# A bidirectional trunk layer on one Trainium2 core: expert weights in 4 MB transfers with eleven chunks fetched ahead, the next gather inside the last down projection, split memory products, narrower clock products

## The reference, cut to what matters

```python
x = LN1(alpha*x + hybrid_mixer(x, w_in, rpb, conv_w, w_out))   # windowed attention + short convolution
x = LN2(alpha*x + memory_cross_attention(x, mem, wq, wk, wv, wo))
x = LN3(alpha*x + expert_choice_moe(x, w_router, w_gate, w_up, w_down))

def memory_cross_attention(x, mem, wq, wk, wv, wo):
    k, v = mem @ wk, mem @ wv                  # (256 x 1024) @ (1024 x 512), twice
...
def expert_choice_moe(x, w_router, w_gate, w_up, w_down):
    affinity = softmax(x @ w_router)           # 512 x 16
    gates, idx = top_k(affinity.T, 64)         # every expert takes its 64 best tokens
    xe = x[idx]                                # 16 x 64 x 1024
    hid = silu(xe @ w_gate) * (xe @ w_up)      # per expert 1024 x 2048, twice
    ye = (hid @ w_down) * gates                # per expert 2048 x 1024
    return scatter_add(idx, ye)
```

## Time and profile before

| | us |
|---|---|
| median of 3 runs | 1283.73 (1283.42 to 1283.82) |
| the profiled execution | 1284.64 |
| its span, first to last instruction | 1282.8 |
| TensorE busy | 1173.8 (92%) |
| VectorE, ScalarE, GpSimd busy | 266.6, 183.3, 117.9 |
| SP's DMA queue, share of 16 engines | 82.0%, 440.84 MB |

### The profile page before, as it was taken

The page is one execution under the profiler, slowest core; times in us unless marked ns, Lnnn a source line. Parts: engine busy times, 40 slices in busy tenths (PEclk is TensorE's granted clock), DMA queues, the critical chain, the costliest instruction groups (busy, mean ns, idle before and its releaser), DMA issues.

```text
span 1282.8 us, 13692 instructions
## 1 busy us (share of the span) xinstructions
PE 1173.8 (92%) x5738; PEld 584.2 (46%) x5738; DVE 266.6 (21%) x488; ACT 183.3 (14%) x338; POOL 117.9 (9%) x59
## 2 busy tenths in 40 slices
PE   8999998999999999999889978997998899789995
PEld 6886776888743343333224322432432243224321
DVE  2012376726710020020002002000200020021114
ACT  4223344133000000000000001000000000000002
POOL 3412324430003000000000000000000000000002
PEclk8999999999999999999999999999999999999998
DMA  9422213048679999999999999999999999999994
GB/s 369 168 87 111 75 69 153 16 199 343 274 287 427 425 428 427 427 430 427 428 429 427 430 428 426 430 428 430 428 427 430 427 427 431 426 429 426 428 426 164
DMA packets 37858, 444.63 MB, mean 347 GB/s; under 512 B 5568, under 2 KB 5952, under 8 KB 10560
## 3 DMA queue, kind: packets, MB, share of 16 engines
q1 hardware_dynamic: 35232, 440.84, 82.0%
q10 hardware_dynamic: 2592, 3.29, 0.8%
HBM read 442.02 MB, written 2.10 MB: 346 GB/s over the span
## 4 chain that ended last, share of the span: by engine, by line
PE 74%; DMA 17%; DVE 5%; ACT 2%; issue 1%; POOL 0%; SPq 0%; DVEq 0%; ACTq 0%
PE bank L1169 25%; DMA ring<-in_w_exp 16%; PE bank L1208 15%; PE bank L1066 5%; PE bank L1218 4%; PE bank L749 2%; PE bank L751 2%; PE bank L754 2%; PE bank L738 2%; ACT yt L694 1%; PE bank L1195 1%; PE bank L1117 1%; PE bank L891 1%; PE bank L893 1%; PE bank L760 1%
## 5 line engine op out<-in xcount | busy, mean ns | idle before, releaser
L1169 PE MATMUL bank<-ring,yt 128*64 128x512 f32 x2048 | 453.1, 595 | 38.0 <-DMA ring<-in_w_exp 38.0
L1169 PEld LDWEIGHTS bank<-ring,yt 128*64 128x64 f32 x2048 | 142.8, 137 | 329.4 <-issue 255.9
L1208 PE MATMUL bank<-ring,yt 128*64 128x512 f32 x928 | 206.6, 596 | 26.7 <-ACT yt L694 20.9
L1208 PEld LDWEIGHTS bank<-ring,yt 128*64 128x64 f32 x928 | 67.0, 137 | 147.6 <-issue 113.9
L1554 DVE TENSOR_TENSOR work<-bank,work 128x512 f32<-128x512 f32 x32 | 22.1, 692 | 422.7 <-PE bank L1169 422.7
L691 ACT ACTIVATE work<-bank 128x512 f32<-128x512 f32 x32 | 19.1, 597 | 534.3 <-PE bank L1169 534.3
L483 POOL TENSOR_TENSOR stat<-stat 128x1 f32<-128x1 f32 x4 | 2.2, 553 | 864.0 <-DVE stat L1583 863.8
L1066 PE MATMUL bank<-yt,res 128*128 128x128 f32 x512 | 61.3, 278 | 11.7 <-DVE yt L1528 11.7
L1066 PEld LDWEIGHTS bank<-yt,res 128*128 128x128 f32 x512 | 58.4, 192 | 24.1 <-DVE xT L1564 15.2
L1564 DVE TENSOR_TENSOR xT<-bank,xT 128x512 f32<-128x512 f32 x56 | 38.7, 691 | 144.3 <-PE bank L1218 144.3
L468 POOL TENSOR_TENSOR piece<-ring,piece 128x1024 fp32r<-128x1024 f32 x23 | 55.1, 2395 | 123.7 <-ACT piece L533 123.7
(11 more groups left out here) (229 smaller groups left out, 1027.0 us busy)
## 6 DMA issues: line engine op xcount, KB each, us to landing
ring<-in_w_exp SPq DMA_DIRECT2D x181, 2048.0 KB, 30.0
ring<-in_dense SPq DMA_DIRECT2D x12, 2048.0 KB, 8.6
ring<-in_w_exp SPq DMA_DIRECT2D x16, 1024.0 KB, 32.9
ring<-in_x_turned SPq DMA_DIRECT2D x8, 256.0 KB, 5.9
res<-in_na_bias SPq DMA_DIRECT2D x1, 2048.0 KB, 23.3
res<-in_x SPq DMA_DIRECT2D x1, 2048.0 KB, 7.7
xT<-in_w_exp SPq DMA_DIRECT2D x1, 2048.0 KB, 14.2
ring<-in_w_exp SPq DMA_DIRECT2D x4, 512.0 KB, 32.3
```

The lines of the kernel that those rows point to most:

```text
L1169: mm = nc.tensor.matmul(bank[2 * g + n % 2][64 * c:64 * c + 64, :], xeT[:, kk, 64 * e:64 * e + 64], exp_rhs(j, first, k, c), start=kk == 0 ...
L1208: mm = nc.tensor.matmul(bank[5][64 * n:64 * n + 64, :], hidT[:, s, 64 * c:64 * c + 64], exp_rhs(j, first, s, n), start=(g, c, s) == (0, 0, ...
```

## The change

- **Transfers.** The host lays two chunks of a pair side by side, so that a partition's run is 32 KB instead of 16 KB. From the second pair on, one DMA brings two chunks (4 MB) into two neighbouring rooms, and waits for both to be free. Of each pair's last two chunks the first 6 rows come in one DMA and the last 2 in another; the last pair keeps its parts of chunks 22 and 23.
- **Ahead of time.** Chunk 2 of the first pair goes into `work` and `ln` in four row DMAs (EARLY), two after the mask's turn and two after the last norm; chunk 4 goes to xT, chunk 9 is the scattered one, and chunk 14 reuses xT. Eleven chunks are loaded ahead. Chunks 11, 12 and 13 come in halves, the first half once half of the room's old chunk is used.
- **Gather.** The gather of pair i + 1 stands in pair i, after the turns of the hidden tile of its second expert: k-tiles 0 to 3, then 4 to 7. VectorE makes the one-hot tiles right after it has kept the scatter tile.
- **Memory products.** They use split pieces as the mixer does: 8 more pieces for ScalarE and GpSimd, plus a split of the memory itself. The loads of chunks 6, 7 and the output weights wait for later pieces accordingly.
- **Clock products.** They are 128 wide instead of 256, and more in number in four of five places.
- **Third norm.** Gain and bias come as single rows by SP; before the last pair TensorE spreads them by four products with a row of ones, and ScalarE copies the four banks to `ln`.

```diff
+EARLY, IN_XT, SCATTERED = 2, (4, 14), 9
+FIRST_SLOT = {0: 0, 1: 1, 3: 2, 5: 3, 6: 4, 7: 5, 8: 6, 10: 7, 11: 0, 12: 1, 13: 2, 15: 3, 16: 4, 17: 5, 18: 6, 19: 7,
+              20: 0, 21: 1, 22: 2, 23: 3}
+IN_HALVES = (11, 12, 13)
...
+            def load_two(j, pair):
+                room, src = exp_room(j), exp_two(pair, j)
+                if j < CPP - 2:
+                    sp.dma_start(room, src).then_inc(two_landed(j), 16)
                     return
+                for rows, landed in ((slice(0, 6), half_in), (slice(6, 8), two_landed(j))):
+                    sp.dma_start(room[:, rows], src[:, rows]).then_inc(landed, 16)
...
+            sp.wait_ge(turned, TN_MASK + 1)
+            sp.wait_ge(above_ready, 1)
+            for row in (0, 1):
+                sp.dma_start(early[row], exp_src(0, EARLY)[:, row, :]).then_inc(early_in, 16)
+            sp.wait_ge(normed, 2 * TT)
+            for row in (2, 3):
+                sp.dma_start(early[row], exp_src(0, EARLY)[:, row, :]).then_inc(early_in, 16)
+            for j in range(FIRST_LOTS, CPP):
+                if j in IN_HALVES:
+                    sp.wait_ge(half_used, IN_HALVES.index(j) + 1)
+                    load_exp(j, slice(0, 2))
+                    sp.wait_ge(exp_used, USED_FIRST[j] + 1)
+                    load_exp(j, slice(2, 4))
+                    continue
+                sp.wait_ge(exp_used, USED_FIRST[j] + 1)
                 load_exp(j)
             with sp.Fori(1, LAST) as i:
-                for j in range(CPP):
-                    sp.wait_ge(exp_used, i * CPP + (j - SLOTS + 1))
-                    load_exp(j, i, first=False)
+                for j in range(0, CPP, 2):
+                    sp.wait_ge(exp_used, i * CPP + (j - SLOTS + 2))
+                    load_two(j, i)
...
-            act.wait_ge(normed, 2 * TT)
-            load_ln(ln3_g, ln3_b)
...
-                    nc.tensor.matmul(pv[0][:, 0:256], ident, cst[:, 0:256], start=True, stop=True)
+                    nc.tensor.matmul(pv[0][:, 0:128], ident, cst[:, 0:128], start=True, stop=True)
...
+            def mem_k(p):
+                pe.wait_ge(hi_split, p)
+                for k in range(KT):
+                    nc.tensor.matmul(acc, hi[:, k, :], m_hi[:, k, :], start=k == 0, stop=False)
+                for k in range(KT):
+                    nc.tensor.matmul(acc, hi[:, k, :], m_lo[:, k, :], start=False, stop=False)
+                pe.wait_ge(lo_split, p)
+                for k in range(KT):
+                    mm = nc.tensor.matmul(acc, lo[:, k, :], m_hi[:, k, :], start=False, stop=k == KT - 1)
...
                         mm.then_inc(hid_turned, 1)
+                        if e and g == 0:
+                            pe.wait_ge(half_picked, i + 2)
+                            pe.wait_ge(mix_kept, i * MIX + 1)
+                            gather(0, 4)
+                        elif e:
+                            gather(4, 8)
                         pe.wait_ge(hidT_kept, i * 4 + (2 * e + g + 1))
...
+                elif j == CPP - 2:
+                    pe.wait_ge(half_in, i * 16)
+                elif j % 2 == 0:
+                    pe.wait_ge(two_landed(j), i * 48 + (16 * (j // SLOTS) - 32))
...
+            pe.wait_ge(ln_in, 32 * 2 + 16 * 2)
+            for a in range(2):
+                for n in range(2):
+                    mm = nc.tensor.matmul(bank[2 * a + n][:, :], cst[0:1, C_ONE:C_ONE + P], ln[0:1, a, 512 * n:512 * n + 512],
+                                          start=True, stop=True)
+            mm.then_inc(ln_wide, 1)
             pair(LAST, last=True)
...
-    return out.reshape(E * CPE, P, SLOT)
+    return out.reshape(E * CPE // 2, 2, P, SLOT).transpose(0, 2, 1, 3).reshape(E * CPE // 2, P, 2 * SLOT)
```

More of the change, by code:

```diff
@@ L26, with place, landings @@
 SLOTS = 8
-FIRST = 3
-EXTRA = 8
-EXTRAS = 2
 CPE = 12
 CPP = 2 * CPE
+EARLY, IN_XT, SCATTERED = 2, (4, 14), 9
+FIRST_SLOT = {0: 0, 1: 1, 3: 2, 5: 3, 6: 4, 7: 5, 8: 6, 10: 7, 11: 0, 12: 1, 13: 2, 15: 3, 16: 4, 17: 5, 18: 6, 19: 7,
+              20: 0, 21: 1, 22: 2, 23: 3}
+FIRST_LOTS = 11
+IN_HALVES = (11, 12, 13)
+RING_AT = 4
+def place(j):
+    return "xT" if j in IN_XT else FIRST_SLOT[j]
+USED_FIRST = {j: max(m for m in range(j) if m not in (EARLY, SCATTERED) and place(m) == place(j))
+              for j in range(FIRST_LOTS, CPP)}
+def landings(j):
+    return sum(2 if m in IN_HALVES else 1 for m in FIRST_SLOT if m <= j and FIRST_SLOT[m] == FIRST_SLOT[j])
 C_ID, C_TRI, C_ONE, C_RANK = 0, 128, 256, 384
@@ L96 @@
 MO_GROUPS = MH
-MIX = 3 + 8
+MIX = 1 + 8
 LAST = PAIRS - 1
@@ L359, in load_pre, with load_exp @@
                 sp.dma_start(pre_flat(c), dense[c]).then_inc(pre_in[PRE_SLOT[c]], 16)
[L361 to L366, removed]
+            def load_exp(j, rows=slice(0, 4)):
+                landed = xT_in if j in IN_XT else exp_in[FIRST_SLOT[j]]
+                sp.dma_start(exp_chunk(j, True)[:, rows], exp_src(0, j)[:, rows]).then_inc(landed, 16)
+            def load_two(j, pair):
+                room, src = exp_room(j), exp_two(pair, j)
+                if j < CPP - 2:
+                    sp.dma_start(room, src).then_inc(two_landed(j), 16)
                     return
-                sp.dma_start(exp_chunk(j, first), exp_src(pair, j)).then_inc(landed, 16)
+                for rows, landed in ((slice(0, 6), half_in), (slice(6, 8), two_landed(j))):
+                    sp.dma_start(room[:, rows], src[:, rows]).then_inc(landed, 16)
             def load_x(k):
@@ new lines, in mem_v @@
+            def mem_v(p):
+                hi, lo = (piece[:, p % 2, h].rearrange("p k n -> p (k n)").rearrange("p (k n) -> p k n", k=2)
+                          for h in range(2))
+                k0 = 2 * (p - MV_PIECES[0])
+                acc = [pj[(PJ_MV + t) % 2][:, :] for t in range(MT)]
+                if k0 == 0:
+                    for t in range(MT):
+                        pe.wait_ge(proj_kept[(PJ_MV + t) % 2], (PJ_MV + t) // 2)
+                pe.wait_ge(hi_split, p)
+                for j in range(2):
+                    for t in range(MT):
+                        for m in (m_hi, m_lo):
+                            nc.tensor.matmul(acc[t], m[:, k0 + j, P * t:P * t + P], hi[:, j, :],
+                                             start=k0 + j == 0 and m is m_hi, stop=False)
+                pe.wait_ge(lo_split, p)
+                last = p == MV_PIECES[-1]
+                for j in range(2):
+                    for t in range(MT):
+                        mm = nc.tensor.matmul(acc[t], m_hi[:, k0 + j, P * t:P * t + P], lo[:, j, :], start=False,
+                                              stop=last and j == 1)
+                        if last and j == 1:
+                            mm.then_inc(projected, 1)
+                if not last:
+                    mm.then_inc(mem_v_used, 1)
@@ L1275, in att_low @@
                     .then_inc(att_kept[hp % 2], 1)
+            for a in range(2):
+                k = slice(4 * a, 4 * a + 4)
+                dve.wait_ge(mem_hi_split, a + 1)
+                nc.vector.tensor_tensor(m_lo[:, k, :], memT[:, k, :], m_hi[:, k, :].bitcast(F32), ALU.subtract)\
+                    .then_inc(mem_lo_split, 1)
             dve.wait_ge(v_used, 4)
```

232 lines of the change are left out of this document (131 added, 101 removed).

## The result

The changed kernel takes 1273.45 us in the median of three runs (1273.28, 1273.45 and 1275.64; a fourth took 2010.13 us at a mean granted clock of 0.557, was disturbed and is left out). The kernel before took 1283.78 beside it. The ratio is 0.9924 [0.9906, 0.9942], a gain of 9 to 10 us; a repeat on another chip gave 1274.06 against 1283.39. I had said 1270.8 (1267.0 to 1280.0): sign and range hold, and the gain is 2.5 to 3.5 us smaller than forecast.

The account below looks back on a forecast made before the run. The expert part was taken as bound by its DMA stream; -5.9 (memory), -3.1 (clock), +0.3 (eleventh chunk, halves), -7.9 (longer runs) and +3.7 (tail) sum to -12.9, from 1283.7 to 1270.8 us, range 1267.0 to 1280.0.

Parts of the forecast that it names:

- The bound: Expert part: as long as its bytes take; stream start, pauses, rate and TensorE's work left at its end move the time.
- Rival B: Every transfer from the second pair on: longer runs are read worse, 7.7 us per 1% of rate; chance 0.03.
- Memory products: Dense part, memory blocks as split products: -5.9 us of TensorE (-7 to -2), first convolution block at about 106.2.
- rival C: Memory split not covered: GpSimd's chain or pauses for both piece buffers eat 4 us, 1274.8; chance 0.10.
- Clock products: Choice of tokens: narrower products bring the swap product 2.75 and the mask's turn 0.35 earlier, -3.1 us (-3.6 to -2).
- feared fall of the clock: TensorE rests between rounds; a granted clock at 1.2 GHz would slow ranks, gather and half of chunk 0: +8 us.
- Eleventh chunk and halves: Stream start 4.6 us better, given back by a 5.3 us pause before chunk 32: +0.3 (-4.6 to +4).
- Rival D: No stall at chunk 32, as gathers hide behind ScalarE and VectorE: -4.6, 1266; chance 0.06.
- Longer runs: Chunks 32 to 189: runs of 32 KB save 12.5 ns per packet, 0.05 us per chunk, -7.9 us (0 to -10).
- The tail: End of the last pair: chunks landing in twos make TensorE wait for chunk 20, +3.7 us.
- the norm's products and copies: Last pair's start, about 5 us: cost 0, as TensorE is ahead of the stream there by its chunk 13.
- The moved gather: Later pairs, led by the stream: moving the gather is worth nothing there.

Follow-up runs that it names:

- singles from chunk 8: The combined kernel with the last pair's single 2 MB transfers starting at chunk 8 instead of 16; 1266.84 us, ratio 0.9867.
- the combined kernel: The changed kernel with the third norm's gain and bias spread by DMA, chunks 32 and 33 alone, last pair's chunks 16 to 21 alone; 1268.07 us, ratio 0.9882.
- singles in the last pair: The changed kernel with chunks 16 to 21 of the last pair in transfers of 2 MB each; 1275.55 us, ratio 0.9931.

## Why the prediction was right, and where it was not

**The bound: right.** The expert part goes at the rate of its bytes until the last pair, and start, pause, rate and tail were the four terms to look at. Rival B, a slower rate, falls with the 432 GB/s.

**Memory products: right.** -5.9 forecast, -6.7 in the profile (105.44 against 112.10), 5.7 by the run with plain products. GpSimd's subtractions did not come late, so rival C falls: the convolution blocks start at 105.44, not behind 109.

**Clock products: right.** -3.1 forecast. The swap product gives 2.6, the turn 0.5, and the way from there to chunk 0 0.3, together 3.4; the run with wide products says 2.8. Of the feared fall of the clock the profiled run has nothing. That of the kernel with singles from chunk 8 has one, not between the rounds but behind the ranks, in the clock products ahead of the gather, as the windows show (after, then singles from chunk 8):

```profile
337.00:349.00 12.00, 11.47 (x94) 10.16 (x94) 5.67 (x13) 0.00 (x0) 0.00 (x0) 1.00 0.99 398
```

```profile
337.00:349.00 12.00, 11.46 (x84) 10.87 (x84) 5.40 (x13) 0.00 (x0) 0.00 (x0) 0.86 0.98 392
```

There chunk 0 starts at 349.43, where the combined kernel, the same up to then, has it at 347.55; that profiled run took 1269.97 and the other three 1266.19 to 1266.97. The price of such a fall is under 2 us, not the 8 that I had set as a bound. Two more of the thirteen traces of changed kernels have one at this place, that without halves and that with clock products of 256 columns (PEclk 0.86 and 0.90 over the same window), so nothing here puts it down to the narrower products.

**Eleventh chunk and halves: right in kind.** The ring was full before chunk 32. The pause cost 3.5 to 5 us where 5.3 were forecast. It resumed at t0 + 114.4, where 114.6 was forecast. That the halves are worth nothing while this pause stands is shown by the run without them. Rival D falls.

**Longer runs: right.** 12.5 ns per packet came out as 14 by the rounded rows (2 x 616 - 1218) and as 12.5 by the packet records (2 x 614.7 - 1216.9). The rate is 432, as forecast. Undoing it costs 5.8 us at the end where 7.9 were forecast. Its trace says why: the seventh pair's scatter comes 5.6 later than in after (1142.70 against 1137.07), of which 0.3 to 0.4 was there at chunk 0. So a chunk costs 0.040 us more, not 0.050, over the 131 chunks or so up to there, and what the rate gives behind that doesn't count, since TensorE sets the end. A chunk gains less than its four packets' fixed times. That fits the busy shares: the packets' times add up to 100.8% of the stretch with short runs and to 100.5% with long ones, so neighbours overlap, and a little more where packets are short. The rule of the Trainium skill ("DMA: Bandwidth & Descriptors", Rules for kernel authors), that 128 partitions and 1 MiB per DMA give the full rate, holds here to about 1%: 428 of 432. Over 158 chunks that last per cent is one of the two largest terms of this change.

**The tail: wrong, and this is the failed step.** The range holds the result, but one term of the sum has the wrong mechanism. The prediction said that the third norm's four products and copies come "at the last pair's start, where TensorE is ahead of the stream by its chunk 13 in any case: 0", and that the tail costs +3.7 by a wait for chunk 20. TensorE is not ahead there any more. The stream's end came forward by 17 us (16.6 by my sum), and TensorE, which before had about 14 us to spare in a pair of 117.6, did not come forward with it. From its last wait at 1106.86 it works through chunks 18 to 23, the moved gather and the scatter, spends 6.0 us on the norm's products and on waiting for their copies (1144.78 to 1150.76), and has 101.8 us of its own left. So there is no wait for chunk 20; instead about 11.5 us of products are left when the stream ends, where I had 9 (5.4 and the 3.7). That is +6 instead of +3.7. The runs bear it out from both sides: singles in the last pair give nothing, spreading the norm by DMA gives 3.0, and with it the waits for data are back on the chain. In that kernel the wait for chunk 20 and the 16.4 us behind it are there as forecast. So the term that failed is the norm's products and copies, put at 0, and not the 3.7. That this kernel's 1271.09 lies 0.3 from my 1270.8 is partly luck, since the start came out 1.3 better and the stream 0.9 worse than I had them.

**The moved gather: right only in part.** I had it as "worth nothing" in later pairs, led by the stream. With the end set by TensorE, the boundary of the last pair counts in full. Undoing the move costs 6.0 us. Hence the tail would have been some 6 us worse but for it, and I had the right sum for this move for a wrong reason.

**The balance.** Forecast for start, stream and tail: -9.0, -7.6, +3.7 = -12.9. Found in the profiled execution: -10.3 for the start, about -6.7 for the stream (17 less 10.3), +6 for the tail, thus -11.0 for TensorE's last down product (1252.54 against 1263.55). The medians gain less, 10.3 and, in the repeat, 9.3, since the profiled run is at the fast end.

**What stays open.** The undone parts cost 5.8 + 5.7 + 2.8 + 6.0 = 20.3 us, and the change gave 9 to 10. The two need not agree. The gather's 6.0 is a loss avoided and no gain over before, where that boundary had slack. The other three, 14.3, are gains of start and stream, and the change itself takes part of them back at its end: by the norm's products (3.0) and the rooms in pairs before chunk 32 (about 1.9). That is a rough balance of terms that were never undone together. What the 4 MB transfers cost through their double rooms is bounded from runs only in places: 1.9 us at chunk 32, and 1.2 us, within the scatter, for chunks 8 to 15 of the last pair. A kernel with single rooms throughout and runs of 32 KB wasn't tried, as a chunk of 2 MB is only 16 KB per partition.

## What to carry to other kernels

When a stream bounds a kernel, work out at its last stage how much compute is left behind it: a faster stream moves the bound to the compute of that stage, and work that was free there (a norm's constants, a gather at a boundary) begins to cost its full price. A ring that is filled faster than it is used turns a head start of the stream over the compute into a pause, so relieve the step that frees the next room before you pay for chunks fetched further ahead. A head start of both, as from shorter dense work, comes through whole. Find the last moment at which the compute engine waits for the stream: what moves the stream ahead of it reaches the end in full, and behind it only compute counts. Here smaller transfers behind that moment gave nothing, and 6 us of work taken off the engine there gave 3.0.

## What the hardware showed that I had not expected

**Waiting for two chunks at once lets the clock fall.** In before TensorE waited some 1.2 us per gate and up chunk; now it waits up to 2.7 us ahead of each two chunks. The timeline of TensorE of the changed kernel:

```profile
611.28 7.09 PE L1265 MATMUL bank<-ring,yt 128*64 128x512 f32 x32 [2.04 <-DMA ring<-in_w_exp]
620.90 8.65 PE L1265 MATMUL bank<-ring,yt 128*64 128x512 f32 x32 [2.54 <-DMA ring<-in_w_exp]
630.70 7.09 PE L1265 MATMUL bank<-ring,yt 128*64 128x512 f32 x32 [1.15 <-DMA ring<-in_w_exp]
640.33 8.78 PE L1265 MATMUL bank<-ring,yt 128*64 128x512 f32 x32 [2.54 <-DMA ring<-in_w_exp]
...
825.03 8.78 PE L1310 MATMUL bank<-ring,yt 128*64 128x512 f32 x32 [1.95 <-DMA ring<-in_w_exp]
```

Behind a wait of 2.54 the same 32 products take 8.65 or 8.78 us instead of 7.09: the granted clock is at the 1.2 GHz level for part of them. Behind 2.04 and 1.15 it is not, but further on it is behind 1.95. The wait's length alone doesn't decide: of eleven waits of 2.5 us or more for a transfer five are followed by a fall, and three falls follow waits of 1.80 to 2.04. What else decides isn't shown. There are nine such falls in the expert part of after, eight of them behind a transfer and one behind the norm's copies, and none in before; their mark in the windows above is a PEclk of 0.97 where before had 1.00. It isn't the size of a transfer that does it: the kernel with 16 KB runs has transfers of 2 MB again, waits for two of them at once, and has eleven falls. The eight cost 1.5 to 1.7 us each on TensorE, and nothing at the end where the stream leads. Where TensorE leads, they do: the last pair's first 48 products take 13.39 us in after, behind 2.35 us of rest for the norm's copies, and 10.45 in the kernel that spreads the norm by DMA. The window over them in after, same columns as above:

```profile
1150.76:1164.15 13.39, 13.39 (x49) 4.46 (x50) 0.00 (x0) 0.00 (x0) 0.00 (x0) 0.78 1.01 432
```

So the norm's four products cost TensorE 5.5 us of its start and 2.9 of clock, 8.4 together, of which 3.0 reached the end before the stream bounded it again.

**A transfer of 4 MB near the end is dear twice on TensorE.** In the combined kernel's last pair, chunks 10 and 11 came 3.22 us late, and their 32 products then took 9.86 us instead of 7.09 (the row is quoted above): 6 us of TensorE for one late transfer. Little of it reached the end: with single transfers there the median is 1.2 us lower.
